# A two-block transformer kernel on one core: products of the normed rows with the input weights made from seven quarter products instead of eight

## The reference, cut to what matters

```python
h = rmsnorm(x, norm_mix_g)                  # 512 x 1024
proj = h @ w_in                             # first block: q, k, v and gate logits
gates = sigmoid(gate_logits + b_gate)
merged = gates[:, :, 0] * (o_a @ w_proj_a) + gates[:, :, 1] * (o_b @ w_proj_b)
x = x + merged @ w_out
x = x + moe_ffn(rmsnorm(x, norm_ffn_g), ...)
for l in range(2):                          # second block
    xn = rmsnorm_2(x, pre_g[l])
    proj = xn @ w_in[l]                     # u, v, z of a gating unit; latents; q, k, v, z; gate logits
    ...
    merged = sum(gates * br, axis=2)
    x = x + rmsnorm_2(merged @ w_out[l], post_g[l])
```

## Time and profile before

| | us |
|---|---|
| median of three runs | 3305.73 |
| lowest, highest | 3305.72, 3313.92 |
| the profiled execution, its own time | 3309.29 |
| its span | 3307.5 |
| TensorE busy | 3086.8 (93%) |
| VectorE busy | 922.3 (28%) |
| ScalarE busy | 752.9 (23%) |
| GpSimd busy | 113.8 (3%) |

### The profile page before, as it was taken

The page is one execution under the profiler, slowest core; times in us unless marked ns, Lnnn a source line. Parts: engine busy times, 40 slices in busy tenths (PEclk is TensorE's granted clock), DMA queues, the critical chain, the costliest instruction groups (busy, mean ns, idle before and its releaser), DMA issues.

```text
span 3307.5 us, 37837 instructions
## 1 busy us (share of the span) xinstructions
PE 3086.8 (93%) x13316; PEld 1684.1 (51%) x13317; DVE 922.3 (28%) x2229; ACT 752.9 (23%) x1491; POOL 113.8 (3%) x132
## 2 busy tenths in 40 slices
PE   7999899986999989899899599898999999989998
PEld 3454654454585555375268445544444445444444
DVE  3450651233212121212221313404211224032112
ACT  2221651111212111212211113414111225141111
POOL 0000000000000000000000000000000000000000
PEclk9999999977999999999999899999999999999999
DMA  4221012245999999999999322021222220112222
GB/s 157 70 77 64 1 39 77 89 191 211 369 384 356 416 415 390 419 369 393 419 414 362 143 94 72 24 72 59 77 75 72 83 92 24 58 45 83 77 76 76
DMA packets 137635, 577.26 MB, mean 175 GB/s; under 512 B 15965, under 2 KB 21341, under 8 KB 87360
## 3 DMA queue, kind: packets, MB, share of 16 engines
q1 hardware_dynamic: 128032, 558.87, 44.5%
q0 software_dynamic: 9504, 17.07, 1.4%
HBM read 572.47 MB, written 20.97 MB: 179 GB/s over the span
## 4 chain that ended last, share of the span: by engine, by line
PE 86%; DVE 5%; DMA 5%; ACT 2%; issue 1%; DVEq 1%; SPq 0%; ACTq 0%; POOLq 0%
PE banks L326 41%; PE banks L1307 12%; PE banks L1283 8%; PE banks L323 7%; PE banks L1257 6%; DMA arena<-in_w_experts 4%; PE banks L623 3%; PE banks L646 2%; PE banks L634 2%; PE banks L270 1%; DVE arena L696 1%; DVE arena L708 1%; PE banks L1236 1%; PE banks L1693 1%; PE banks L975 0%
## 5 line engine op out<-in xcount | busy, mean ns | idle before, releaser
L326 PE MATMUL banks<-arena 128*128 128x512 f32 (+2 forms) x3264 | 1391.2, 586 | 7.6 <-DVEq L200 4.9
L326 PEld LDWEIGHTS banks<-arena 128*128 128x128 f32 x3264 | 616.0, 190 | 736.6 <-issue 727.8
L1307 PEld LDWEIGHTS banks<-arena 128*128 128x128 f32 x3584 | 404.1, 193 | 14.5 <-issue 14.5
L1307 PE MATMUL banks<-arena 128*128 128x128 f32 x3584 | 405.8, 276 | 4.8 <-issue 4.8
L1283 PE MATMUL banks<-arena 128*64 128x512 f32 (+1 forms) x1024 | 322.6, 593 | 0.0
L1257 PE MATMUL banks<-arena 128*64 128x512 f32 x1152 | 265.1, 610 | 23.5 <-DMA arena<-in_w_experts 20.9
L323 PE MATMUL banks<-arena 128*128 128x512 f32 x512 | 220.9, 592 | 1.8 <-DVEq L200 1.8
L1385 DVE TENSOR_TENSOR arena<-banks,arena 128x512 f32<-128x512 f32 x64 | 44.3, 692 | 614.9 <-PE banks L1307 352.2
L1283 PEld LDWEIGHTS banks<-arena 128*64 128x64 f32 (+1 forms) x1024 | 123.4, 159 | 176.2 <-issue 176.1
L876 DVE TENSOR_TENSOR arena<-banks,arena 128x512 f32<-128x512 f32 x64 | 44.3, 692 | 515.2 <-PE banks L326 515.2
L1257 PEld LDWEIGHTS banks<-arena 128*64 128x64 f32 x1152 | 83.4, 139 | 188.1 <-issue 186.8
(11 more groups left out here) (211 smaller groups left out, 1865.9 us busy)
## 6 DMA issues: line engine op xcount, KB each, us to landing
arena<-in_w_experts SPq DMA_DIRECT2D x384, 1024.0 KB, 18.7
arena<-in_w_in SPq DMA_DIRECT2D x84, 1024.0 KB, 5.0
arena<-in_w_out SPq DMA_DIRECT2D x12, 1024.0 KB, 5.0
arena<-in_w_branch SPq DMA_DIRECT2D x24, 512.0 KB, 3.5
arena<-expert_rows SPq DMA_DIRECT2D x4, 2048.0 KB, 14.5
arena<-in_w_in SPq DMA_DIRECT2D x4, 832.0 KB, 4.6
arena<-in_gate_b SPq DMA_DIRECT2D x2, 1536.0 KB, 6.7
arena<-in_x SPq DMA_DIRECT2D x4, 512.0 KB, 5.0
```

Of the source, the lines that this page charges most:

```text
L326: last = PE.matmul(PS[:, tt, 0:ncols], lhsT(kk, tt), Wh[h][:, q, 0:ncols], start=(kk == 0), stop=(kk == kt - 1))
L1307: last = PE.matmul(PS[:, q, f * P:(f + 1) * P], gate_up(q, k)[:, f * P:(f + 1) * P], xT[:, k], start=(f == 0 and k == 0), stop=(f == 3 and ...
```

## The change

A product of matrices in quarters takes eight quarter products. The class `Quarters` uses seven, with four sums or differences S1 to S4 of quarters of hT, four differences T1 to T4 of quarters of the weights, and sums at the end. VectorE makes S1 to S4 once for each normed x (for the merge of block one again, since hT was reordered). GpSimd makes T1 to T4 for each product. A quarter product is eight matmuls (two token tiles or weight slices by four contraction blocks) of 256 columns. ScalarE copies four intermediate results out of banks 0, 2, 0, 0 into "parts", and VectorE adds these to what is in the banks and writes the four quarters of the result. `part_mm` counts quarter products, `part_out` the copies, `mixed_w` and `mixed_h` the T's and S's, `ev` the results. Wh[0] and Wh[1] are now given back by GpSimd (`w0_free`, `mm`).

```diff
+            def sums_dve(self, dve):
+                for name, x, y, op in (("S1", "A21", "A22", ALU.add), ("S2", "S1", "A11", ALU.subtract),
+                                       ("S4", "A12", "S2", ALU.subtract), ("S3", "A11", "A21", ALU.subtract)):
+                    V.tensor_tensor(self.a(name), self.a(x), self.a(y), op).then_inc(SEM["mixed_h"], 1)
+                    V.drain()
+            def pool(self, pool, c, k, f, n=512):
+                T, F, w = c.of("T") + k, c.of("F") + f, n // 2
+                def mix(name, x, y, last_use):
+                    pool.wait_ge(SEM["part_mm"], up(7 * (F - 1) + last_use))
+                    G.tensor_tensor(self.b(name, w), self.b(x, w), self.b(y, w), ALU.subtract).then_inc(SEM["mixed_w"], 1)
+                    return G.drain()
+                pool.wait_ge(SEM["w0_in"], 16 * T + 16)
+                mix("T1", "B12", "B11", 3)
+                pool.wait_ge(SEM["w1_in"], 16 * T + 16)
+                mix("T2", "B22", "T1", 4)
+                mix("T3", "B22", "B12", 6)
+                pool.wait_ge(SEM["part_mm"], up(7 * F + 1))
+                G.drain().then_inc(SEM["w0_free"], 1)
+                mix("T4", "B21", "T2", 7)
+                pool.wait_ge(SEM["part_mm"], up(7 * F + 5))
+                G.drain().then_inc(SEM["mm"], 4)
+            def pe(self, pe, c, k, f, n=512, across=False, hooks={}):
...
+                pe.wait_ge(SEM["w0_in"], 16 * T + 16)
+                pe.wait_ge(SEM["part_out"], up(4 * F))
+                product(0, "A11", "B11", 0, True, False)
+                pe.wait_ge(SEM["w1_in"], 16 * T + 16)
+                product(1, "A12", "B21", 1, True)
...
+                product(2, "S1", "T1", 2, True, False)
...
+                pe.wait_ge(SEM["part_out"], up(4 * F + 1))
+                product(3, "S2", "T2", 0, False, False)
+                pe.wait_ge(SEM["part_out"], up(4 * F + 2))
+                product(4, "S4", "B22", 2, False)
+                pe.wait_ge(SEM["part_out"], up(4 * F + 3))
+                product(5, "S3", "T3", 0, False)
+                pe.wait_ge(SEM["ev"], up(4 * T))
+                product(6, "A22", "T4", 3, True)
+            def act(self, act, c, k, f, i, n=512, across=False):
+                bank, after, read = ((0, 1, 3), (2, 3, 1), (0, 4, 2), (0, 6, 0))[i]
+                act.wait_ge(SEM["part_mm"], up(7 * F + after))
+                AC.activation(v(self.parts[i], 2 * w), PS[:, bank, 0:2 * w], ACT.Copy).then_inc(SEM["part_out"], 1)
+            def dve(self, dve, c, k, f, i, dst, n=512, across=False):
+                bank, after, put = ((1, 2, 1), (2, 5, 3), (None, 6, 4), (3, 7, 4))[i]
+                dve.wait_ge(SEM["part_mm"], up(7 * F + after))
+                dve.wait_ge(SEM["part_out"], up(4 * F + put))
+                one = self.part(1, w) if bank is None else of(bank)
+                V.tensor_tensor(to, one, self.part((0, 2, 3, 3)[i], w), ALU.add).then_inc(SEM["ev"], 1)
```

In `qk_tile` ScalarE's program for a product becomes this (VectorE makes results 0 and 1, then tiles 0 and 1, results 2 and 3, then tiles 2 and 3):

```diff
+                Q1.act(act, c, k, k, 0, n)
+                back(0)
+                back(1)
+                Q1.act(act, c, k, k, 1, n)
+                back(2)
+                Q1.act(act, c, k, k, 2, n)
+                back(3)
+                square(0)
+                square(1)
+                root(0)
+                Q1.act(act, c, k, k, 3, n)
+                root(1)
+                for tt in (2, 3):
+                    square(tt)
+                    root(tt)
```

More of the change, by code:

```diff
@@ L462, in act_, with back, square @@
+                Q1.pe(pe, c, k, k, n, hooks=hooks)
             def act_(act, c):
-                for tt in range(TT):
+                def back(tt):
                     if prev:
                         tr_out(act, "act", c, 4 * (k - 1) + tt, prev["dst"](c, k - 1, tt), prev["cnt"])
-                    act.wait_ge(SEM["mm"], up(unit(c, k, tt)))
-                    apart(act, unit(c, k, tt))
-                    AC.activation(ST[tt][:, 0:cfg["ncols"]], PS[:, tt, 0:cfg["ncols"]], ACT.Copy)
+                def square(tt):
+                    act.wait_ge(SEM["ev"], up(unit(c, k, 1 if tt < 2 else 3)))
@@ L528, in build @@
                  "gain": lambda c, k: v(GAINS + 7 * E, E)}
-        QKC = {"tr": 4, "T": 1, "qk_ms": 4, "qk_sd": 4, "qk_ready": 4, "tile": 1}
+        QKC = {"tr": 4, "T": 1, "F": 1, "qk_sq": 4, "qk_ms": 4, "qk_sd": 4, "qk_ready": 4, "tile": 1}
+        PARTS2 = [GAINS, MASKA + 1024, GROW + 1024, CO["ropeB_c"]]
+        Q1 = Quarters([OA + 1024 * i for i in range(4)], VA, [VA + 4096 + 512 * i for i in range(4)], 0)
         def constants():
@@ L1779, in dve_ @@
+                for tt in (2, 3, 0, 1):
+                    act.wait_ge(SEM["ev"], up(unit(c, 0, 2 if tt > 1 else 3)))
+                    AC.activation(v(YC + 512 * tt, 512), v(SC + 512 * tt, 512), ACT.Sigmoid).then_inc(SEM["z_sig"], 1)
+                for k in range(1, 4):
+                    act0(act, c, k, 0, 1, 2, 3)
             def dve_(dve, c):
-                for q in range(4):
-                    dve.wait_ge(SEM["ev"], up(unit(c, 3, q)))
+                dve0(dve, c, 0, v2(SC, TT, 512), 0, 1, 2, 3)
@@ L1782, in dve_, with pool_ @@
+                for n, q in enumerate((2, 3, 0, 1)):
+                    dve.wait_ge(SEM["z_sig"], up(6 * c.of("layer") + 3 + n))
                     V.tensor_tensor(v(YC + 512 * q, 512), v(YC + 512 * q, 512), v(SC + 512 * q, 512), ALU.mult)
-            heads = Stage({"T": 4}, sp=sp_, pe=pe_, act=act_, dve=dve_, lead=lead, pool=lambda pool, c: biases(pool, c, (0, 1)))
+                for k in range(1, 4):
+                    dve0(dve, c, k, v2(CQK + 2048 * (k - 1), TT, 512), 0, 1, 2, 3)
+            def pool_(pool, c):
+                pool0(pool, c, (0,))
+                biases(pool, c, (0,))
+                pool0(pool, c, (1,))
+                biases(pool, c, (1,))
+                pool0(pool, c, (2, 3))
```

310 lines of the change are left out of this document (197 added, 113 removed).

## The result

| | before | changed |
|---|---|---|
| median of four runs each, us | 3309.82 | 3267.12 |
| lowest to highest | 3305.72 to 3318.47 | 3262.25 to 3275.76 |
| profiled execution, us (its span) | 3309.29 (3307.5) | 3275.76 (3273.9) |
| mean granted TensorE clock in it | 0.970 | 0.960 |

The ratio is 0.9866, with an interval of 0.985 to 0.9883: less time by 43 us or 1.3%, clear of no change, where 51 us were forecast.

What follows compares the result with a forecast made beforehand. TensorE, busy for 93% of the span, was taken as the bound. -134.4 + 30.4 + 23.4 + 7.6 + 7.5 + 13 + 1.4 = -51 us gave 3258 for the profiled execution, 3255 us for the median; range 3208 to 3294.

Steps and rivals of the forecast that it cites:

- TensorE's work: All quartered products: 112 half-wide records of 0.216 us, 24.20 us for a full product; -134.4 us in sum.
- The gates' weights: Gate products: TensorE waits 1.9 us for the second half of the weights in each of 16; +30.4 us.
- The query loop: Query and key products: GpSimd's differences hold VectorE 5.2 us, TensorE waits 3.9 us in six intervals; +23.4 us.
- first rival: Query loop: GpSimd does not hold up VectorE's two-input operations; 3214 us, chance 0.23.
- only behind that root stands ScalarE's first copy, for which quarter product 3 waits: Query loop: the copy after tile 3's root ends at 16.85 us and closes a loop of 24.6 us without GpSimd.
- The clock, +7.5: Query loop: TensorE's clock falls after waits of 3.9 us, 2.5 us charged for half of the six.
- KB, +7.6: Product behind QB: KB ends 31 us after QB's quarter product 4 where TensorE needs 21.2.
- 2.2 of this wait is there today: KB: 2.2 us of its wait was taken to exist already in the kernel before.
- The starts, +13: Three starts: 1 to 2 us each for S1, 8 us at block two's first product, 3 us in layer two.
- The second: Rival: the clock falls at the gates' 16 short waits and all six query waits, 47.5 us more; 3303 us, chance 0.08.
- The third: Rival: GpSimd far slower, 7 us for a difference; 3385 us, gain used up from about 4 us; chance 0.08.

Runs made afterwards that it cites:

- experiment 7: Changed kernel with the third quarter product ahead of the second in the merges: 3232.6 us, ratio 0.9765.
- experiment 1: Changed kernel with GpSimd's differences cut to 8 of 1024 elements in query and key products behind the first: 3275.7 us, loop period 25.99 us.
- experiment 2: Changed kernel with those differences replaced by GpSimd zero fills that only write: 3265.16 us, loop period 25.98 us.
- experiment 3: Changed kernel with those differences replaced by two GpSimd copies of one input: mean loop period 28.3 us, read in the stage alone.
- experiment 4: Changed kernel with every GpSimd difference made twice in the same products, same result: 3315.46 us, ratio 1.0006.
- experiment 5: Changed kernel with ScalarE's first copy for the next query product moved ahead of the root of tile 3: 3260.49 us, ratio 0.9853.
- experiment 6: Changed kernel with that ScalarE copy moved and the previous tile's transposes put behind later quarter products: 3241.31 us, ratio 0.9787.
- the kernel with all edits: Changed kernel with copy and turns moved, third quarter product ahead of second in merges, and GpSimd waiting for block two's norm: 3200.87 us, ratio 0.9665.
- experiment 8: Changed kernel with GpSimd waiting at block two's two starts until VectorE has normed all four tiles: 3255.81 us, ratio 0.9821.

## Why the prediction was right, and where it was not

**TensorE's work: exact.** Four products in a row of the chunked attention take 96.95 us, 24.24 each, where 24.20 was worked out and four took 110.1 before; a quarter product is 3.47. The weight loads stay covered, though their count rises with the matmuls' (PEld 1684 to 2072 us).

**The gates' weights: right.** 16 waits with 28.7 us in the waits' view against 30.4, and by experiment 7, which takes them away, 31 to 35. In one the clock fell as well: the last gate product of merge 1 waited 3.57 us, and its 96 records took 23.95 instead of 21.0. That is most of what merge 1 is short of its forecast. The load for this product landed 6.95 us behind the branch product's end, where the others took 4.9 to 5.4; SyncE issues five smaller loads for the next stages right behind it. That these delay it was not tested.

**The query loop: the right holder, the right price, and one of two links.** GpSimd's reads hold VectorE's two-input operations for the whole of an instruction, the point that the forecast rested on and its first rival denied; experiments 1 to 4 settle it. The price was 2.35 us against 2.1 taken, and VectorE's waits were 4.9 us against 5.2, though partly at other operations than forecast: T2 held the last sum of tile 0, T3 the mean and T4 the second multiplication. The loop was forecast at 29.8 us without the clock and came to 30.3 with it. But the step "only behind that root stands ScalarE's first copy, for which quarter product 3 waits" named only one of two links. The transposes of tile 1 stand in front of it, TensorE waits there for 2.0 to 2.5 us in all six periods, and by experiments 5 and 6 the copy alone gives 3 us of the stage, copy and turns together 24. The working had the length of the chain of VectorE and did not ask where each tile's end is waited for.

**The clock, +7.5: right in kind, counted in the wrong manner.** The 24 records behind the wait of 2.00 us took 7.04 instead of 5.2. So it went behind four of the six waits, of 2.47, 2.07, 2.38 and 2.00 us, and not behind 2.33 and 1.99; three had been charged. The records run while ScalarE and VectorE go on, so what the slower TensorE loses lies almost wholly inside the wait for the copy that comes next. The periods show it: with the slow stretch they are 30.20, 30.52 and 30.14 us, and with the clock up and a wait of 1.7 us for the copy 30.45 and 30.12. So the two do not add as the sum has them, and the term of 7.5 us stands for a cost that the loop hardly shows. Up to KB's beginning the queries cost 4.3 us in each period over 25.98, 25.9 in six, where 30.9 were forecast for loop and clock.

**KB, +7.6: too low.** From KB's beginning (230.4 in the changed kernel, from the pieces of the chain) to its end are 26.3 us, where it was 15.6 before: +10.8, against +6.3 forecast (7.6 less the 1.3 of its smaller work). Half of the miss is a reading: "2.2 of this wait is there today" is in no row, since before, TensorE runs through KB without a gap, and 15.6 us are its work and four transposes. The other half is the length, 33.3 us from QB's quarter product 4 to KB's end instead of 31. With the thin differences of experiment 1 it is still 24.5. So GpSimd has little to do with it. TensorE's waits in KB are 4.2 us for VectorE's last operation of a tile of QB and 4.0 for a copy of ScalarE: its quarter products of 1.8 us are too short for the copies and for the tiles of QB that are to be turned between them. No experiment takes these two apart. The two misses cancel: the stage was forecast at +14.9 and came to +15.6. The sum was right there, its parts were not.

**The starts, +13: right in size.** Behind products that gained 9.8 us each, block two's stage gained 1.1 and layer two's 4.2, so the starts cost 8.7 us (forecast 8) and 5.6 (3), each with its wait for S1. These waits, for which 2 us were left, were 0.3 to 0.4 us at each of the three starts.

**What was missed.** Set against the profile of before, the forecast was 3258 us, and the profiled execution took 3275.76, of which 9 us are its distance from the median. The largest part of the 17 us lies in the chunked attention of the layers, 7; merge 1 has 5, the experts 3. Around the four products stands work that the change does not touch. Ahead of them it took 83.5 and 86.5 us in the two layers before, and 85.5 and 88.4 after; behind them 54.1 and 54.6 before, and 56.9 and 53.8 after, 6 us more in all. Two of these windows of layer one, first of the kernel before (ahead of the products), then of the changed kernel:

```profile
2036.17:2119.62 83.45, 71.64 (x417) 45.41 (x417) 46.33 (x173) 46.69 (x127) 0.00 (x0) 0.96 0.03 12
```

```profile
2048.49:2134.00 85.51, 74.44 (x416) 46.70 (x417) 46.34 (x173) 46.80 (x127) 0.00 (x0) 0.92 0.00 1
```

Behind the products, in the changed kernel:

```profile
2230.95:2287.86 56.91, 43.59 (x321) 28.39 (x321) 36.15 (x151) 32.81 (x91) 8.21 (x12) 0.85 0.02 6
```

and in the kernel with all edits:

```profile
2191.32:2245.10 53.78, 41.05 (x320) 25.98 (x321) 36.16 (x151) 32.58 (x91) 8.22 (x12) 0.90 0.02 6
```

In the last two the matmuls, VectorE's and ScalarE's work are the same, and 3.1 us lie between them, with the granted clock at 0.85 and 0.90. Before, the four windows had 0.96, 0.91, 0.90 and 0.91, in the changed kernel 0.92, 0.85, 0.86 and 0.90. So the chunked attention's gain of 27 us arrived as 20. Which execution and which stretch get the lower clock changes in the same code: in the kernel of experiment 8 the four have 0.94, 0.91, 0.98 and 0.85. Whether the change makes the lower one likelier stays open, with one profile of the kernel before.

**The rivals.** The first (no hold, 3214 us) falls by experiments 1 to 4. The second (the clock falls at the short waits too) was true of one gate wait, of 3.57 us, and not of the other 15: their 96 records take 20.99 to 21.05 us. The third's mechanism is the one of experiment 4, and its turning point, 4 us for a difference, was measured as just under 4.7 with the other products left at 2.35.

The Trainium skill, SBUF — State Buffer, section "Who interferes with whom", has three rules that these traces bear out. A GpSimd instruction that only writes does not contend with VectorE's two-input form (experiment 2: 693 ns). `tensor_scalar` can contend, when it enters a mode that uses both ports (0.76 instead of 0.17 us beside a fill). And `tensor_reduce` never contends on trn2: it takes 681 to 684 ns on average in every kernel here, whatever GpSimd does.

## What to carry to other kernels

Work given to GpSimd is not beside VectorE's: as long as it reads SBUF, it takes the time of VectorE's two-input and scalar operations, so price it on VectorE, and look at what stands on the bounding engine behind VectorE at that moment. Smaller pieces on TensorE shorten the cover of every load and of every hand-over; move the piece that needs least ahead, and the turns and copies behind pieces that can run without them, as two of the three edits did; with the third, GpSimd kept out of the norm, they brought 66 us, more than the change itself. When an experiment changes data that steer later work, read it by the stage.

## What the runs showed of the hardware that I had not expected

- VectorE's `tensor_scalar` on 8 elements, 0.17 us alone, took 1.72 us beside a difference on GpSimd and 0.76 beside a plain fill: the smallest operations are held up as long as the large.
- GpSimd is held as well. At the start of block two, beside VectorE's additions of 1024 elements, its differences took 2.46, 3.07 and 3.12 us, where 2.35 is their usual time.
- Halving the width of an fp32 matmul to 256 columns, with a new weight load each time, halves the time of a record: 0.216 us against 0.429.
- The granted clock fell behind waits as short as 2.00 us in the query loop (0.79 in the window of 147 to 155 us), while it had been 1.00 behind 1.8 us.
